# Banded attention in an encoder trunk: turned probabilities as stationary operand, values streamed, division behind the product

## What is computed

```python
scores = einsum(q, kb) * HEAD_DIM ** -0.5          # bands of 3 blocks of 128 keys
scores = where(valid, scores - slopes * dist, NEG_BIG)
m = maximum(max(scores, -1), sink)
p = exp(scores - m)
probs = p / (sum(p, -1) + exp(sink - m))
out = einsum(probs, vb)
return out.reshape(B, S, N_HEADS * HEAD_DIM) @ w_o
```

## Time and profile before

| | |
|---|---|
| median of 3 runs (3077.0 to 3077.72) | 3077.22 us |
| the profiled execution's own time; its span | 3077.01 us; 3075.2 us |
| TensorE busy, share of the span | 2920.1 us, 95% |
| DVE, ScalarE, GpSimd | 1681.1 us, 786.5 us, 986.1 us |
| mean granted TensorE clock | 0.976 |
| attention loop, first scores to the out projection | 1708.8 to 1979.1 us |
| ScalarE's high part of a unit; issue of a gain row's DMA | 0.59 us; 0.46 us |
| gain and shift rows scaled, DVE's first residual tile | 2000.95 us |

### The profile page before, as it was taken

The page is one execution under the profiler, slowest core; times in us unless marked ns, Lnnn a source line. Parts: engine busy times, 40 slices in busy tenths (PEclk is TensorE's granted clock), DMA queues, the critical chain, the costliest instruction groups (busy, mean ns, idle before and its releaser), DMA issues.

```text
span 3075.2 us, 36198 instructions
## 1 busy us (share of the span) xinstructions
PE 2920.1 (95%) x14070; PEld 2386.1 (78%) x14070; DVE 1681.1 (55%) x2708; ACT 786.5 (26%) x1731; POOL 986.1 (32%) x817
## 2 busy tenths in 40 slices
PE   8999959889999999999899899898999999999996
PEld 7888847778888888888688544576788888888884
DVE  3689963674444444444720698666743444444447
ACT  3221342421111111112221466404211111111121
POOL 3355402362233223323131333224532233223323
PEclk9999979999999999999899899999999999999998
DMA  4000003111111111111121000211111111111111
GB/s 128 28 26 16 28 1 117 28 39 30 42 42 37 32 42 42 35 42 35 62 71 30 21 1 1 86 42 28 42 41 29 41 42 38 31 42 42 37 36 72
DMA packets 156950, 124.69 MB, mean 41 GB/s; under 512 B 27953, under 2 KB 133849, under 8 KB 156792
## 3 DMA queue, kind: packets, MB, share of 16 engines
q1 hardware_dynamic: 149736, 96.85, 11.2%
q10 hardware_dynamic: 7056, 25.69, 2.2%
HBM read 112.03 MB, written 10.49 MB: 40 GB/s over the span
## 4 chain that ended last, share of the span: by engine, by line
PE 85%; DVE 10%; ACT 4%; issue 1%; DMA 0%; POOL 0%; POOLq 0%; DVEq 0%; SPq 0%; ACTq 0%
PE bank L638 26%; PE bank L633 26%; PE bank L636 25%; PE bank L990 3%; PE bank L966 2%; DVE conv_acc L1356 2%; PE bank L981 1%; DVE stats L1286 1%; ACT y L1147 1%; PE bank L665 1%; ACT gained_tile L1035 1%; DVE y L1303 1%; DVE y L1305 1%; ACT probs L1236 1%; DVE y L1572 1%
## 5 line engine op out<-in xcount | busy, mean ns | idle before, releaser
L633 PE MATMUL bank<-x_hi,w_hi 128*128 128x498 f32 (+3 forms) x2688 | 962.1, 358 | 39.1 <-DVE up_conv L1480 18.1
L638 PE MATMUL bank<-x_hi,w_lo 128*128 128x498 f32 (+3 forms) x2688 | 962.7, 358 | 0.0
L636 PE MATMUL bank<-x_lo,w_hi 128*128 128x498 f32 (+3 forms) x2688 | 958.8, 357 | 0.0
L546 POOL CAST w_hi<-raw_pieces 128x512 fp32r<-128x512 f32 x348 | 341.9, 983 | 1750.2 <-issue 1253.3
L633 PEld LDWEIGHTS bank<-x_hi,w_hi 128*128 128x128 f32 x2688 | 508.8, 189 | 111.4 <-issue 30.2
L636 PEld LDWEIGHTS bank<-x_lo,w_hi 128*128 128x128 f32 x2688 | 507.4, 189 | 70.7
L638 PEld LDWEIGHTS bank<-x_hi,w_lo 128*128 128x128 f32 x2688 | 506.9, 189 | 69.4
L550 POOL TENSOR_TENSOR w_lo<-raw_pieces,w_hi 128x512 fp32r<-128x512 f32 x348 | 479.6, 1378 | 27.9
L1474 DVE SCALAR_TENSOR_TENSOR gate_conv<-bank,ffn_conv_table,gate_conv 128x496 f32<-128x496 f32 (+2 forms) x176 | 92.7, 547 | 613.5 <-ACT up_conv L1173 610.0
L1513 DVE TENSOR_TENSOR y<-y,bank 128x512 f32<-128x512 f32 x440 | 298.2, 685 | 225.4 <-PE bank L638 220.5
L1173 ACT ACTIVATE gate_conv<-bank,ffn_conv_table 128x497 f32<-128x497 f32 x132 | 93.6, 709 | 969.2 <-PE bank L638 969.2
(11 more groups left out here) (147 smaller groups left out, 3707.3 us busy)
## 6 DMA issues: line engine op xcount, KB each, us to landing
raw_pieces<-in_ffn_w_up_dram SPq DMA_DIRECT2D x168, 256.0 KB, 2.9
raw_pieces<-in_ffn_w_down_dram SPq DMA_DIRECT2D x84, 256.0 KB, 2.6
raw_pieces<-in_conv_w_pw_dram SPq DMA_DIRECT2D x48, 256.0 KB, 2.7
y<-in_x_prompt_dram ACTq DMA_DIRECT2D x16, 512.0 KB, 6.4
residual_dram<-y ACTq DMA_DIRECT2D x10, 512.0 KB, 2.7
y<-residual_dram ACTq DMA_DIRECT2D x10, 512.0 KB, 9.6
out_dram<-y SPq DMA_DIRECT2D x10, 512.0 KB, 2.6
raw_pieces<-in_attn_w_q_dram SPq DMA_DIRECT2D x32, 128.0 KB, 2.4
```

The costliest lines, as they stand in the source:

```text
L546: pool.tensor_copy(WH[:, p % RING, :], raw[:, p % RAW, :]).then_inc(piece_hi, 1)
L633: mm = pe.matmul(out, left[0], right[0], start=first, stop=False)
L636: pe.matmul(out, left[0], right[1], start=False, stop=False)
L638: return pe.matmul(out, left[1], right[0], start=False, stop=last)
```

## The change

The value product swaps its operands: a turned block of probabilities of one head (128 keys x 128 queries) is stationary and V (64 columns) is streamed, so that the result lies with the queries on the partitions. There the division by the sum is one small multiplication behind the product, and the normalisation of the probabilities goes. In return the result must be turned, four 128x128 transposes for half a tile, through bank 7, and is then split into `x_hi` and `x_lo`. The ring of turned blocks has six places, in the last 256 columns of the memory of `x_hi` and `x_lo`; the value product of a unit now starts when all its blocks are copied. Banks 0 and 1 alone hold scores. The heads' results overwrite q in `y`, whose layout is now by tile. Tiles 0 to 7 are turned inside the loop (`heads_step`), tiles 8 and 9 between steps of the out projection's first block, and a tile's residual is reloaded when it is turned. The negative maximum takes two small steps instead of three.

```diff
+        with ExitStack() as a:
+            probsT_first = sb("probs_T_first", [P, KT, T], where=a)
+            probsT_last = sb("probs_T_last", [P, KT, T], where=a)
...
-        q_sb = conv
+        q_sb = y[:].rearrange("p n (c t) -> p n c t", t=P)
+        heads = y[:].rearrange("p n (k s d) -> p n k s d", s=2, d=HD)
...
-        SCORE_BANKS = (0, 1, 7)
+        UNIT_OF = [i for i, (n, _, _) in enumerate(ATT) for _ in key_blocks(n)]
+        SCORE_BANKS = (0, 1)
+        KEY_RING = 6
+        TURNED_LATE = (TT - 2, TT - 1)
+        def probs_turned_block(u):
+            v = u % KEY_RING
+            whole, k = (probsT_first, 2 * v) if v < KT // 2 else (probsT_last, 2 * v - KT)
+            return whole[:, k:k + 2, S0:S0 + 2 * P].rearrange("p k (r t) -> p k r t", t=P)
+        def av_bank(i):
+            return bank[5 + i % 2][:, 0:GROUP * HD]
+        def heads_step(i):
+            return [(n, half) for n in range(TT) if n not in TURNED_LATE for half in range(2)
+                    if i == 4 * n + 4 + 2 * half]
...
-            for i in range(len(ATT)):
-                if i < RING - 1:
-                    stretch(B_O + i, B_O + i + 1)
-                normalise_half(i)
-            stretch(B_O + RING - 1, B_FFN1)
+            ffn_stretch(B_O, B_FFN1)
...
-                    if u >= 3:
-                        pe.wait_ge(score_kept, u - 2)
+                    if u >= 2:
+                        pe.wait_ge(score_kept, u - 1)
...
+            def turn_heads(n, half):
+                pe.wait_ge(heads_ready, 4 * n + 4)
+                if n or half:
+                    pe.wait_ge(heads_lo, 2 * n + half)
+                for k in range(4):
+                    mm = pe.transpose(bank[7][:, cols(k)], y[:, n, cols(4 * half + k)], ident[:])
+                mm.then_inc(heads_turned, 1)
...
-                pe.wait_ge(probs_ready, i + 1)
-                pe.wait_ge(probs_ready_pool, i + 1)
+                pe.wait_ge(exp_ready, i + 1)
...
                 if i + 3 < len(ATT):
                     scores(i + 3)
+                for m, half in heads_step(i):
+                    turn_heads(m, half)
                 if i >= 2:
-                    pe.wait_ge(av_lo, i - 1)
+                    pe.wait_ge(heads_ready, i - 1)
                 g = 2 * rr + par
-                for j, b in enumerate(kb):
-                    pe.wait_ge(probs_T_kept, KEYS_TO[i] + j + 1)
-                    pe.matmul(bank[5 + i % 2][0:HD, :], v_sb[:, b, g * HD:(g + 1) * HD],
-                              probsT[:, (KEYS_TO[i] + j) % 2, :], start=(j == 0), stop=(j == len(kb) - 1)
-                              ).then_inc(av_done, 1)
-            pe.wait_ge(av_lo, len(ATT))
-            out_projection(B_O, 1)
+                pe.wait_ge(probs_T_kept, KEYS_TO[i + 1])
+                for r in range(GROUP):
+                    for j, b in enumerate(kb):
+                        mm = pe.matmul(av_bank(i)[:, r * HD:(r + 1) * HD],
+                                       probs_turned_block(KEYS_TO[i] + j)[:, r // 2, r % 2, :],
+                                       v_sb[:, b, g * HD:(g + 1) * HD], start=(j == 0), stop=(j == len(kb) - 1))
+                mm.then_inc(av_done, 1)
+            late = [(n, half) for n in TURNED_LATE for half in range(2)]
+            pe.wait_ge(score_kept, GROUP * len(ATT))
+            out_projection(B_O, 1, lambda k: turn_heads(*late[k]) if k < len(late) else None, (heads_lo, 2 * TT))
...
+            def heads_high(n, half):
+                act.wait_ge(heads_turned, 2 * n + half + 1)
+                act.activation(XH[:, 4 * half:4 * half + 4, cols(n)],
+                               bank[7][:].rearrange("p (k t) -> p k t", t=P), ACT.Copy).then_inc(heads_hi, 1)
+                if half:
+                    act.dma_start(y[:, n, :], residual_rows[n]).then_inc(res_landed[n], 16)
...
-                    if u >= 2:
-                        act.wait_ge(av_done, u - 1)
-                    act.activation(probsT[:, u % 2, :], bank[2 + j][:, :], ACT.Copy).then_inc(probs_T_kept, 1)
-                act.wait_ge(av_done, KEYS_TO[i + 1])
-                act.activation(XH[par * HD:(par + 1) * HD, GROUP * rr:GROUP * (rr + 1), cols(n)],
-                               bank[5 + i % 2][0:HD, :].rearrange("p (k t) -> p k t", t=P), ACT.Copy
-                               ).then_inc(av_hi, 1)
+                    if u >= KEY_RING:
+                        act.wait_ge(av_done, UNIT_OF[u - KEY_RING] + 1)
+                    act.activation(probs_turned_block(u), bank[2 + j][:].rearrange("p (k r t) -> p k r t", k=2, t=P),
+                                   ACT.Copy).then_inc(probs_T_kept, 1)
                 if i + 3 < len(ATT):
                     exponentials(i + 3)
-            act.wait_ge(av_lo, len(ATT))
-            for t in range(TT):
-                act.dma_start(y[:, t, :], residual_rows[t]).then_inc(res_landed[t], 16)
+                for m, half in heads_step(i):
+                    heads_high(m, half)
+            act.wait_ge(av_done, len(ATT))
+            for n in TURNED_LATE:
+                for half in range(2):
+                    heads_high(n, half)
...
+            def keep_heads(i):
+                n, rr, par = ATT[i]
+                dve.wait_ge(av_done, i + 1)
                 dve.wait_ge(recip_ready, i + 1)
+                dve.tensor_tensor(heads[:, n, GROUP * rr:GROUP * (rr + 1), par, :],
+                                  av_bank(i).rearrange("p (r d) -> p r d", d=HD),
+                                  srec[:, i % 3, :].unsqueeze(2).to_broadcast([P, GROUP, HD]), ALU.mult
+                                  ).then_inc(heads_ready, 1)
...
             for i in range(3):
                 biased_scores(i)
-            normalise(0)
+            denominators(0)
             for i in range(len(ATT)):
                 if i + 1 < len(ATT):
-                    normalise(i + 1)
+                    denominators(i + 1)
                 if i + 3 < len(ATT):
                     biased_scores(i + 3)
                 if i >= 1:
-                    heads_low(i - 1)
-            heads_low(len(ATT) - 1)
+                    keep_heads(i - 1)
+                    for n, half in heads_step(i - 1):
+                        heads_low(n, half)
+            keep_heads(len(ATT) - 1)
+            for n in TURNED_LATE:
+                for half in range(2):
+                    heads_low(n, half)
```

More of the change, by code:

```diff
@@ L275, in trunk @@
         av_done = sem("av_done")
-        av_hi = sem("av_hi")
-        av_lo = sem("av_lo")
+        heads_ready = sem("heads_ready")
+        heads_turned = sem("heads_turned")
+        heads_hi = sem("heads_hi")
+        heads_lo = sem("heads_lo")
         block = ctx.enter_context(nc.Block())
@@ L776, in _, with out_projection @@
                 mm.then_inc(ct_turned, 1)
-            def out_projection(base, use, between=None):
+            def out_projection(base, use, between, between_done):
                 norm = 2 * use
@@ L799, in out_projection @@
                                     mm.then_inc(proj_done, 1)
-                            if between and n == 0 and t0 == 0:
+                            if n == 0 and t0 == 0:
                                 between(k)
@@ L805, in out_projection @@
                                 turn_tile(norm + 1, turns[t0, k])
-                        if between and n == 0 and t0 == 0:
-                            pe.wait_ge(silu_lo, TT)
+                        if n == 0 and t0 == 0:
+                            pe.wait_ge(*between_done)
             for t in range(BLOCKS[0][1]):
@@ L963, in scores @@
                     u = GROUP * i + r
-                    if u >= 3:
-                        pe.wait_ge(score_kept, u - 2)
-                    pe.matmul(bank[SCORE_BANKS[u % 3]][:, 0:len(kb) * P], q_sb[half, GROUP * rr + r, cols(n)],
+                    if u >= 2:
+                        pe.wait_ge(score_kept, u - 1)
+                    pe.matmul(bank[SCORE_BANKS[u % 2]][:, 0:len(kb) * P], q_sb[half, n, GROUP * rr + r, :],
                               k_sb[half, rr, kb[0] * P:(kb[-1] + 1) * P], start=True, stop=True
                               ).then_inc(score_done, 1)
+            def turn_heads(n, half):
[5 more added lines that the diff above has]
+                mm.then_inc(heads_turned, 1)
             pe.wait_ge(qkv_kept, unit)
@@ L1210, in keep @@
                 act.wait_ge(qkv_done, unit + 1)
-                act.activation(out, bank[2 + unit % 2][:, 0:n], ACT.Copy, scale=scale).then_inc(qkv_kept, 1)
+                source = bank[2 + unit % 2][:, 0:n]
+                if len(out.shape) == 3:
+                    source = source.rearrange("p (b t) -> p b t", t=P)
+                act.activation(out, source, ACT.Copy, scale=scale).then_inc(qkv_kept, 1)
                 unit += 1
@@ L1586, in _ @@
                                      op1=ALU.max).then_inc(vec_step, vs.one())
```

(22 more changed lines are left out.)

34 lines of the change are left out of this document (6 added, 28 removed).

## The result

The changed kernel takes 3197.18 us (median of 4 runs, 3184.74 to 3198.33) against 3077.47 us in the runs beside it: a ratio of 1.0377, 95% interval 1.0359 to 1.0395. That is 119.7 us more, where I had said 57. The direction was right, the size was half of it, and the time lies outside the range.

The account below looks back on a forecast made before the run. TensorE was taken to set the attention loop's period. The terms 8 + 10 + 26 + 14 + 4 - 4 + 0 = 58 us (unrounded 57), on 3077.2 us, gave 3134 us; range for 8 in 10: 3090 to 3160.

Parts of the forecast that it names:

- The price of the new product: Value product: 832 records at 0.125 us; inner unit 3.0 us against 2.82, units with two key blocks 2.0 against 1.84.
- step (3): Turn of each tile's first half waits for DVE's kept heads: eight TensorE stalls of 3.45 or 2.7 us, 26 us.
- The turns: Turning the result: 80 additional TensorE transposes of 0.122 us, 9.8 us; the other engines' work lies beside TensorE.
- the stage behind the loop: Out projection after the attention loop: as before; the prediction is wrong if it changes by more than 3 us.
- A: Value product: load and stream don't overlap at 64 columns, 0.18 us a record; 46 us more, 3180 us; chance 0.08.
- B: Turns in the loop: the stall for kept heads is small; 40 us less, 3094 us; chance 0.08.
- C: Value product: records come 0.062 us apart; 52 us less, rings give back some 12, 3094 us; chance 0.07.
- D: Value product: record costs its stream alone, 0.053 us; 60 us less, 3074 or 3060 us; chance 0.05.
- step (4): TensorE's clock after each of eight stalls: 1.7 us lost each, 14 us in all; bounds 0 and 4.5 each.
- (6): Loop start: first transposes need not wait for normalised rows, DVE's first three units as serial as before; -4 us (-2 to -8).
- step (1): Score banks 3 to 2: third score waits for DVE, 0.12 us a unit; unit periods give +7 and +1 us.
- (5): ScalarE's high part and residual DMA issue ahead of copies: a tile's last unit late by 0.35 to 1.0 us; 4 us.

Follow-up runs that it names:

- run 9: Changed kernel with one line moved: DVE keeps the heads of unit i - 1 before taking the scores of unit i + 3; 3125.82 us, ratio 1.0157.
- run 5: Changed kernel with turns one unit later (no stalls) and V streamed 128 columns wide instead of 64, half unread; 3091.58 us, ratio 1.0046.
- the square: Four kernels, without or with stalls: old value product 3093.6 and 3134.6 us, new product 3134.3 and 3197.2 us (the last is the changed kernel).
- run 2: Changed kernel, stalls kept, with the value product in its old form (V stationary, 512 columns streamed; result not the attention's); 3134.6 us, ratio 1.0178.
- run 1: Changed kernel with every turn of a half tile one unit later, so no stalls; 3134.31 us, ratio 1.0171.
- run 6: Changed kernel, stalls included, with V streamed 128 columns wide instead of 64, half unread; 3132.14 us, ratio 1.0168.
- Run 7: Kernel before the change with two score banks instead of three and nothing else; 3095.92 us, ratio 1.0052.
- Run 3: Changed kernel with turns one unit later and the value product in its old form (result not the attention's); 3093.59 us, ratio 1.0043.
- run 8: Kernel before the change with 28 unread products of 512 columns where TensorE waits at the attention loop's start; 3074.71 us, ratio 0.9989.

## Why the prediction was right and wrong

**Right.** TensorE bounds the loop, and the change gives it more to do. The price of the new product at full clock held: 0.112 us a record against my 0.125, near the lower bound of 0.105 from the loads. The stall of step (3), its place, its number and its length held (24.0 us against 26), and run 9 shows its cause. The turns were 80 transposes; the stage behind the loop changed by 2.5 us. Rivals A (no overlap), B (no stall), C and D (cheaper records) are all refuted by these rows. The 81 ns that the Trainium skill (TensorE: Matmul & The Clock Gate, Back-to-back issue gap) gives for load and matmul pairs of 128 columns did not show; run 5 has such pairs at 0.116 us.

**Wrong: step (4), the clock.** I put it at 14 us, 1.7 us for each of eight idle times, with 4.5 each as the bound; it cost about 80 (103.6 in the square less the 24.0 of the waits). The 1.7 came from the earlier trace rows, and both rows stand before products of 498 and 256 columns. So I took what brings the clock back for granted. With the old product the price per stall was nearly right: the loop of run 2 lost 0.08 x 321.8 = 26 us to the clock, less the 8 of before, over eight stalls 2.2 us each, and the square gives 2.1 (17.0 / 8). With the new one it was not the stalls alone: 40.7 us are lost without any (run 1), and the start, which I had left at "as before" in (6), remained at 1.2 GHz to about 1794 us in the changed kernel (to 1732 in the kernel before). I had noticed the halved column count and used it only for rival D, as a possible gain. It was the loss. Runs 5 and 6 show it by themselves: twice the columns in the same records brought back 42.7 and 65 us.

**Mis-sized: step (1), the banks.** I had 0.12 us a unit from one hand-drawn turn, 3 us in 24 units; it is 0.34 in inner units. The 0.85 us from a score's start to its use stands in no row of mine for 384 columns: the earlier trace rows have 1.01 (1801.86 to 1802.87), the changed kernel 1.02. And I left out the way back: after TensorE has waited for DVE, DVE waits for TensorE. For the two-key units the terms that I listed add up to 7.48 us, not 7.65. Run 7, in which nothing else changes, makes the third bank worth 16 us, but with DVE's normalisation still in its way at the start; in the changed kernel it is less. Run 3 is only 14 us above the kernel before with the banks, the 10 us of turning and the quicker start together, which leaves some 7 for the banks and the late units of (5), where I had 12. No run isolates (5).

Step (6) forecast a gain of 4 us at the start, and most of it came: the first transposes begin at 1720.20 us instead of 1722.89, and run 3 is still 2.9 us ahead at unit 4 (1747.78 against 1750.71). The changed kernel has lost it by unit 2 (1740.09 against 1737.93), at half clock. The 4 us of run 8 are another gain, that of a start at full clock.

What stays open: the three-key units of run 1 keep the full clock with the same product with which the two-key units lose it, and no run shows what in the unit makes that difference; the columns of the transposes and of the scores were never changed. Nor does a run show whether the short wait of 0.36 us starts the fall in run 1. That filling the stalls themselves would keep the clock was not tried.

## What to carry to other kernels

Where short streams make a product load-bound, price it twice: once by time a record, and once by the granted clock, because a TensorE that is busy with loads can be given half the clock (here for 40 us on end in the two-key units, though not in the three-key units of run 1). If the record's time is set by the load, try to widen the stream until it fills it: here the columns cost 0.004 us a record and were worth 43 to 65 us. And when a wait is moved, read the other engine's program for what stands ahead of the instruction that ends it.

## What was not expected of the hardware

TensorE at 1.2 GHz for 40 us on end while its busy share was 40.00 of 40.00 us. The Trainium skill (TensorE: Matmul & The Clock Gate, Part 1: The HAM clock gate) lets the clock follow how busy the engine was; by the busy time of the trace the clock should have been full there, so what the trace counts as busy can't be what decides alone. The same page (HAM oscillation) puts the loss of the clock down to idle gaps, there waits for a DMA; run 1 fell with no idle time over 0.36 us ahead of it, and run 5, with 0.31 us at the same kind of place and twice the columns, did not.

The fall also hides itself. At half clock the units last so long that the waits for ScalarE are gone: the table of waits of the changed kernel shows 2.4 us for its copies where the kernel before had 6.4, and looks the healthier of the two.
